# Expert lists of 32 tokens on four column strips in place of 64 tokens on two, in a fused float32 mixture-of-experts block

## The reference

```python
def hier_moe(x, w_group, b_group, w_expert, b_expert, w1, w3, w2):   # 256 tokens
    g_prob = softmax(x @ w_group + b_group)            # 4 groups, the best one is taken
    e_logits = (x @ w_expert + b_expert)               # 8 experts in that group, the best two are taken
    ...
    gates = sum(one_hot(expert_id, 32) * weight)       # two experts of 32 for each token
    def step(acc, ew):                                 # for each of the 32 experts
        h = silu(x @ w1e) * (x @ w3e)                  # 1024 -> 512
        return acc + ge[:, None] * (h @ w2e)           # 512 -> 1024
```

## Time and profile before

| | |
|---|---|
| median of 3 runs | 2823.86 us (2822.52 to 2825.3) |
| span of the profiled execution | 2819.0 us (no time of its own is given beside the span; the runs lie 3.5 to 6.3 us above it) |
| TensorE matmul busy | 2512.3 us, 89% |
| VectorE, ScalarE, GpSimd busy | 800.3, 628.9, 164.9 us |
| read from memory | 598.25 MB, of which expert weights 192 transfers of 2048 KB |
| experts, first layer | first up product at 248.05 us, last scatter ends at 795.21 us |
| experts, second layer | first up product at 1032.52 us, last scatter ends near 1531.9 us |

### The profile page before, as it was taken

One profiled execution on the slowest core, in us unless ns is written; L12 is line 12 of the kernel. 1 busy time (PEld: TensorE's weight loads), 2 busy tenths in 40 slices (PEclk: granted clock), 3 DMA queues, 4 the chain that ended last, 5 costly groups with the idle time before them and its releaser, 6 DMA issues.

```text
span 2819.0 us, 30761 instructions
## 1 busy us (share of the span) xinstructions
PE 2512.3 (89%) x12481; PEld 1598.0 (57%) x12482; DVE 800.3 (28%) x1338; ACT 628.9 (22%) x1012; POOL 164.9 (6%) x90
## 2 busy tenths in 40 slices
PE   7878999999979979999897897898999968878998
PEld 6544444444356644443333785556887847744996
DVE  1252011010020221011002546524232326354444
ACT  1121010101000610111102312423222224224334
POOL 0000000000000000000000325000000004240000
PEclk9988999999989989999999988899999988789999
DMA  8675976999966669999999001300323140130351
GB/s 326 260 276 187 393 286 231 393 393 394 396 250 243 233 242 385 394 393 393 395 396 359 1 1 60 123 1 22 113 90 120 45 163 1 60 117 7 135 199 71
DMA packets 241920, 602.27 MB, mean 214 GB/s; under 512 B 12679, under 2 KB 21751, under 8 KB 241824
## 3 DMA queue, kind: packets, MB, share of 16 engines
q1 hardware_dynamic: 241824, 600.91, 56.7%
HBM read 598.25 MB, written 2.64 MB: 213 GB/s over the span
## 4 chain that ended last, share of the span: by engine, by line
PE 70%; SPq 14%; DVE 6%; DMA 4%; ACT 2%; issue 2%; POOL 1%; DVEq 0%; ACTq 0%; POOLq 0%
PE ps L1756 13%; SPq L647 13%; PE ps L752 10%; PE ps L1565 8%; PE ps L1772 7%; PE ps L759 6%; PE ps L214 4%; PE ps L735 3%; PE ps L727 3%; PE ps L223 3%; PE ps L1738 3%; DMA ring<-in_moe_w_dram 1%; PE ps L1689 1%; PE ps L1709 1%; PE ps L313 1%
## 5 line engine op out<-in xcount | busy, mean ns | idle before, releaser
L752 PE MATMUL ps<-ring,arena 128*64 128x512 f32 x2176 | 477.2, 595 | 20.6 <-DMA ring<-in_moe_w_dram 18.7
L1756 PE MATMUL ps<-ring_r,ring_r 128*128 128x512 f32 (+1 forms) x2112 | 372.1, 339 | 12.5 <-DVE ring_r L2090 12.5
L1756 PEld LDWEIGHTS ps<-ring_r,ring_r 128*128 128x128 f32 x2112 | 329.0, 192 | 54.8 <-DVE ring_r L2090 13.1
L752 PEld LDWEIGHTS ps<-ring,arena 128*64 128x64 f32 x2176 | 155.9, 137 | 335.1 <-issue 305.8
L759 PE MATMUL ps<-ring,arena 128*64 128x512 f32 x1088 | 248.5, 598 | 26.8 <-ACT arena L817 13.8
L1565 PE MATMUL ps<-ring_r,ring_r 128*128 128x512 f32 (+2 forms) x1056 | 217.7, 367 | 8.9 <-DVE ring_r L1975 8.9
L1289 POOL TENSOR_TENSOR ring_r<-ring,ring_r 128x1024 fp32r<-128x1024 f32 (+2 forms) x28 | 85.9, 3088 | 2180.6 <-ACT ring_r L1284 2180.6
L1565 PEld LDWEIGHTS ps<-ring_r,ring_r 128*128 128x128 f32 x1056 | 189.1, 212 | 37.4 <-issue 9.3
L1772 PE MATMUL ps<-ring_r,ring_r 128*128 128x512 f32 x480 | 157.4, 401 | 12.3 <-DVE arena_r L1332 12.3
L759 PEld LDWEIGHTS ps<-ring,arena 128*64 128x64 f32 x1088 | 76.4, 137 | 151.2 <-issue 130.3
L907 DVE TENSOR_TENSOR arena<-ps,arena 128x512 f32<-128x512 f32 x34 | 23.6, 693 | 470.0 <-PE ps L752 470.0
(11 more groups left out here) (321 smaller groups left out, 2500.1 us busy)
## 6 DMA issues: line engine op xcount, KB each, us to landing
ring<-in_moe_w_dram SPq DMA_DIRECT2D x192, 2048.0 KB, 19.3
ring<-in_w_mod_dram SPq DMA_DIRECT2D x24, 2048.0 KB, 13.5
ring<-in_w_gate_dram SPq DMA_DIRECT2D x10, 2048.0 KB, 9.1
ring<-in_w_up_dram SPq DMA_DIRECT2D x10, 2048.0 KB, 14.2
ring<-in_w_in_dram SPq DMA_DIRECT2D x8, 2048.0 KB, 14.8
ring<-in_w_down_dram SPq DMA_DIRECT2D x8, 2048.0 KB, 11.4
ring<-in_w_out_dram SPq DMA_DIRECT2D x4, 2048.0 KB, 10.1
ring<-in_w_down_dram SPq DMA_DIRECT2D x4, 1536.0 KB, 8.1
```

The costliest lines, as they stand in the source:

```text
L752: ins = pe.matmul(PS[CAP * e:CAP * e + CAP, 2 + c, :], xeT[:, k, CAP * e:CAP * e + CAP], w[c][:, e, k, :], start=(k == 0), stop=(k == KT - 1))
L1756: ins = pe.matmul(PS[:, 2 * (i % GU_BANKS) + a, 0:ntok], w[:, k, a, :], as_r(x[:, k, 0:ntok]), start=(k == 0 and n == 0), stop=(k == KT - ...
```

## The change

A round takes 32 tokens of each expert (`CAP = 32`). The up product has 32 stationary columns for each expert, and its 512 output columns are split into two halves of 256, so that two experts x two halves lie on four column strips of 32. The down product splits its 1024 output columns likewise into two halves of 512 on four strips, so `down` is one stage and Y is 128 x 512. The scatter has one strip of 32 rows (an expert and a half) for each product: four products at a time go to four banks, then, behind a wait for a semaphore (`scattered`), four more with the two experts exchanged. `gather` moves 64 columns in place of 128, writes one bank, and stands ahead of the whole down product. ScalarE alone copies `xeT`, VectorE alone copies `Y`. `rounds` has four comparisons more (up to 8 rounds of 32 in place of 4 of 64).

```diff
-    CAP = 64
+    CAP = 32
+    HALF = HIDDEN // 2
...
-            def scatter(last=False):
-                for tt in range(NT):
-                    for h in range(2):
-                        ins = pe.matmul(PS[:, 4 + 2 * tt + h, :], sgT[:, tt * P:(tt + 1) * P], Y[:, h * 512:(h + 1) * 512],
+            def scatter(strips, last=False):
+                for tt, e in enumerate(strips):
+                    for o in range(2):
+                        at = 64 * e + 32 * o
+                        ins = pe.matmul(PS[:, 4 + 2 * tt + o, :], sgT[at:at + 32, tt * P:(tt + 1) * P], Y[at:at + 32, :],
...
-                        ins = pe.matmul(PS[:, 2 + k // 4, (k % 4) * P:(k % 4 + 1) * P], X[:, tt, k * P:(k + 1) * P],
-                                        view(sel[:, tt, 0, 0:1], [1, P]), start=(tt == 0), stop=(tt == NT - 1))
+                        ins = pe.matmul(PS[:, 2, 2 * CAP * k:2 * CAP * (k + 1)], X[:, tt, k * P:(k + 1) * P],
+                                        view(sel[:, tt, 0, 0:1], [1, 2 * CAP]), start=(tt == 0), stop=(tt == NT - 1))
...
                         for e in range(2):
-                            ins = pe.matmul(PS[CAP * e:CAP * e + CAP, 2 + c, :], xeT[:, k, CAP * e:CAP * e + CAP], w[c][:, e, k, :],
+                            for o in range(2):
+                                at = 64 * e + 32 * o
+                                ins = pe.matmul(PS[at:at + CAP, 2 + c, 0:HALF], xeT[:, k, CAP * e:CAP * e + CAP],
+                                                w[c][:, e, k, o * HALF:(o + 1) * HALF], start=(k == 0), stop=(k == KT - 1))
...
-                scatter()
+                scatter((0, 1)).then_inc(s("scattered"), 1)
                 for tt in range(NT):
-                    ins = pe.transpose(PS[:, 0, tt * P:(tt + 1) * P], selg[:, tt, :], ident)
+                    ins = pe.transpose(PS[:, 0, tt * P:(tt + 1) * P], view(selg[:, tt, 0, 0, 0:1], [1, P]), ident)
                 ins.then_inc(s("sgT_ps"), 1)
+                pe.wait_ge(s("scattered"), g * 2 + (2 * layer + 1))
+                scatter((1, 0)).then_inc(s("scattered"), 1)
                 pe.wait_ge(s("h"), g + 1)
-                for k in range(4):
+                for k in range(2):
                     ins = pe.transpose(PS[:, 1, k * P:(k + 1) * P], hh[:, k * P:(k + 1) * P], ident)
                 ins.then_inc(s("hT_ps"), 1)
+                pe.wait_ge(s("sel"), g + (2 + layer))
+                gather()
                 pe.wait_ge(s("sgT"), g + (2 + layer))
                 pe.wait_ge(s("hT"), g + 1)
                 arrived(2)
-                down(0)
-                pe.wait_ge(s("sel"), g + (2 + layer))
-                gather()
-                down(1).then_inc(s("y"), 1)
+                down().then_inc(s("y"), 1)
...
                 act.wait_ge(s("sgT_ps"), g + (2 + layer))
+                act.wait_ge(s("scattered"), g * 2 + (2 * layer + 2))
                 act.copy(sgT, PS[:, 0, 0:256]).then_inc(s("sgT"), 1)
...
-                dve.tensor_tensor(hh, PS[:, 3, :], hs, ALU.mult).then_inc(s("h"), 1)
+                dve.tensor_tensor(hh, PS[:, 3, 0:HALF], hs, ALU.mult).then_inc(s("h"), 1)
...
-                dve.tensor_copy(Y[:, 512:D], PS[:, 1, :]).then_inc(s("y_dve"), 1)
+                dve.tensor_copy(Y, PS[:, 0, :]).then_inc(s("y_sb"), 1)
```

More of the change, by code:

```diff
@@ L629, in moe @@
         pm, rounds, base = area(16), area(16), area(17)
-        sel = area(256).rearrange("p (t e c) -> p t e c", t=NT, e=2)
-        selg = area(256).rearrange("p (t s) -> p t s", t=NT)
+        sel = area(2 * 2 * CAP).rearrange("p (t e c) -> p t e c", t=NT, e=2)
+        selg = area(256).rearrange("p (t e o c) -> p t e o c", t=NT, e=2, o=2)
         sgT = area(256)
[L633 to L636, removed]
+        xeT = area(KT * 2 * CAP).rearrange("p (k s) -> p k s", k=KT)
+        hs, hh = area(HALF), area(HALF)
+        hT = area(HALF).rearrange("p (j s) -> p j s", j=2)
+        Y = area(512)
         st = small[:, 192:204]
@@ L754, in up, with down @@
                     ins.then_inc(s(("h1", "h3")[c]), 1)
-                def down(h):
+                def down():
                     for k in range(4):
                         for e in range(2):
-                            ins = pe.matmul(PS[CAP * e:CAP * e + CAP, h, :], hT[:, k, CAP * e:CAP * e + CAP],
-                                            w[2][:, e, k, h * 512:(h + 1) * 512], start=(k == 0), stop=(k == 3))
-                    return ins
-                pe.wait_ge(s("xe_act"), g + 1)
@@ L763, in body @@
-                pe.wait_ge(s("xe_dve"), g + 1)
+                            for o in range(2):
+                                at = 64 * e + 32 * o
+                                mid = 64 * e + 32 * (k // 2)
+                                ins = pe.matmul(PS[at:at + CAP, 0, :], hT[:, k % 2, mid:mid + CAP],
+                                                w[2][:, e, k, o * 512:(o + 1) * 512], start=(k == 0), stop=(k == 3))
+                    return ins
+                pe.wait_ge(s("xe_sb"), g + 1)
@@ L764, in body @@
                 up(0)
                 up(1)
-                pe.wait_ge(s("y_act"), g + (1 + layer))
-                pe.wait_ge(s("y_dve"), g + (1 + layer))
-                scatter()
+                pe.wait_ge(s("y_sb"), g + (1 + layer))
+                scatter((0, 1)).then_inc(s("scattered"), 1)
                 for tt in range(NT):
-                    ins = pe.transpose(PS[:, 0, tt * P:(tt + 1) * P], selg[:, tt, :], ident)
+                    ins = pe.transpose(PS[:, 0, tt * P:(tt + 1) * P], view(selg[:, tt, 0, 0, 0:1], [1, P]), ident)
@@ L778, in body @@
                 arrived(2)
-                down(0)
-                pe.wait_ge(s("sel"), g + (2 + layer))
-                gather()
-                down(1).then_inc(s("y"), 1)
+                down().then_inc(s("y"), 1)
             pe.wait_ge(s("ctrl"), layer + 1)
-            for b in range(2):
-                ins = pe.matmul(PS[:, b, :], zeros[:, 0:P], zeros, start=True, stop=True)
-            ins.then_inc(s("y"), 1)
+            pe.matmul(PS[:, 0, :], zeros[:, 0:P], zeros, start=True, stop=True).then_inc(s("y"), 1)
             if layer:
@@ L794, in pe_ @@
             total = pe.value_load(ctrl[0:1, cB + PAIRS:cB + PAIRS + 1], min_val=1, max_val=128)
-            pe.wait_ge(s("y_act"), total + (1 + layer))
-            pe.wait_ge(s("y_dve"), total + (1 + layer))
-            scatter(last=True).then_inc(s("done"), 1)
+            pe.wait_ge(s("y_sb"), total + (1 + layer))
+            scatter((0, 1), last=True).then_inc(s("scattered"), 1)
+            pe.wait_ge(s("scattered"), total * 2 + (2 * layer + 1))
+            scatter((1, 0), last=True).then_inc(s("scattered"), 1)
         def act_(act):
@@ L898, in body @@
                 for tt in range(NT):
-                    ins = dve.tensor_tensor(selg[:, tt, :].rearrange("p (e c) -> p e c", e=2), sel[:, tt],
-                                            view(gates[:, tt, bass.ds(pair, 2)], [1, 2], [0, CAP]), ALU.mult)
+                    ins = dve.tensor_tensor(selg[:, tt], view(sel[:, tt, 0, 0:1], [CAP, 2], [0, 2], [1, CAP]),
+                                            view(gates[:, tt, bass.ds(pair, 2)], [1, 2], [0, 2], [0, CAP]), ALU.mult)
                 ins.then_inc(s("sel"), 1)
-                dve.wait_ge(s("xe"), g * 2 + (2 * layer + 2))
-                dve.tensor_copy(view(xeT[:, 4, 0:1], [1, 512]), PS[:, 3, :]).then_inc(s("xe_dve"), 1)
                 y_copy(g)
@@ L906, in body @@
                 dve.wait_ge(s("h3"), g + 1)
-                dve.tensor_tensor(hh, PS[:, 3, :], hs, ALU.mult).then_inc(s("h"), 1)
+                dve.tensor_tensor(hh, PS[:, 3, 0:HALF], hs, ALU.mult).then_inc(s("h"), 1)
             def y_copy(g):
                 dve.wait_ge(s("y"), g + (1 + layer))
-                dve.tensor_copy(Y[:, 512:D], PS[:, 1, :]).then_inc(s("y_dve"), 1)
+                dve.tensor_copy(Y, PS[:, 0, :]).then_inc(s("y_sb"), 1)
             for_rounds(dve, body)
             dve.memset(tm, 0.0).then_inc(s("sel"), 1)
-            y_copy(dve.value_load(ctrl[0:1, cB + PAIRS:cB + PAIRS + 1], min_val=1, max_val=128))
+            total = dve.value_load(ctrl[0:1, cB + PAIRS:cB + PAIRS + 1], min_val=1, max_val=128)
+            y_copy(total)
             dve_layer_norm(dve, link, lambda tt, h: PS[:, 4 + 2 * tt + h, :],
-                           lambda e, tt, h: e.wait_ge(s("done"), layer + 1),
+                           lambda e, tt, h: e.wait_ge(s("scattered"), total * 2 + (2 * layer + 2)),
                            lnp[:, 0:D], lnp[:, D:2 * D], lambda e: e.wait_ge(S("ln_in1"), 32 * layer + 32), (xr, st), ln_tag)
```

19 lines of the change are left out of this document (6 added, 13 removed).

## The result

The kernel after takes 2832.84 us (median of 9 runs, 2827.2 to 2837.37) against 2823.16 us (9 runs). The ratio is 1.0034, with a 95% interval of [1.0024, 1.0043]: 9.7 us slower. A second series of 12 runs on another chip gives 1.0035 [1.0024, 1.0046]. The profiled span is 2828.7 us in place of 2819.0.

What follows compares the result with a forecast made beforehand. It took transfers (32 us) to bound pairs of one round, TensorE (59.5 us) pairs of two. Holes +10.8, starts -6.7, ends -19.6 and 5c of 6 gave -9.5: 2823.9 becomes 2814 us, range 2801 to 2846.

Steps and rivals of the forecast that it cites:

- the sum: Whole kernel: holes +10.8, layer starts -6.7, layer ends -19.6, plus 5c: -15.5 + 5c, or -9.5 us.
- rival 2: Each round 1 to 2 us longer, by late `sel` or slow instruction issue: 2830 to 2846 us, chance 0.19.
- One round: First `up` product to the next round's on TensorE: 17.6 us in place of 29.75.
- rival 1: Scatter row strips don't run together: round 22.4 us, +67 in all, about 2891 us, chance 0.09.
- Number of rounds: Lists over 32 tokens take more rounds: 43 in both layers in place of 34.
- Holes of the first layer: Transfer gaps behind pairs 4, 5 and 6: 57.2 + c us in place of 47.
- c: Delay when TensorE's clock has fallen while it waited for weights: taken as 1.2 us, bounds 0 and 3.
- Holes of the second layer: Transfer gaps at second pairs of two rounds (8 and 11), none at single ones: 2.6 + 2c us.
- The ends of the layers: Last w2 to last scatter's end: 7.4 + c us in place of 17.2, twice.
- The clock: TensorE's clock falls while idle; third rival, in each wait: c 2.5 to 3, total -3 to 0 us, chance 0.12.

Runs made afterwards that it cites:

- a_straight: The kernel after with TensorE's code written out for all 16 pairs in both layers, no jump back: 2815.77 us against 2823.88 before, ratio 0.9973.
- a_straight_again: The kernel after with TensorE's code written out for all 16 pairs, run again on another chip: 2818.77 us against 2822.74 before, ratio 0.9988.
- b_loop8: The kernel before with TensorE's loop over 8 pairs written out in place of 4, no other change: 2831.14 us, ratio 1.0036.

## Why the prediction was wrong

The forecast was 2814 us (-9.5), measured was +9.7. Two terms of the sum failed, both in the second layer: the jump of TensorE's loop, which it left out (point 3), and the holes behind pairs of two rounds, which it put at 5 us (point 5). By its terms the first layer should have changed by -0.6 us, and its stretch changed by -1.0; the second by -9.0, and it changed by +9.9. The time lies in the range of rival 2 (2830 to 2846), but not for its reason: no round got longer.

1. **One round: right, slightly too dear.** 17.04 us against 17.6. Row strips at 1.07 us (the lower bound 1.06; I took 1.2), one `up` pair 6.91, `gather` 3.68, `down` 3.57. By the page's factor of 3.07 (the Trainium skill, "TensorE: Matmul & The Clock Gate", Measured speedup vs the span model) a half would be 1.12 us; the row agrees within 0.05. Row strips do run together, so rival 1 did not occur, and the round is shorter than forecast, so neither did rival 2.
2. **Number of rounds: right**, 43.
3. **The sum left out the jump of TensorE's loop.** This is the first step that failed. I counted every product and weight load (424 for a round in place of 284) and asked only whether they could be issued fast enough, not what it costs to go back over them. Undone in both layers it gives 17 us in one series and 13 in another (1.0034 to 0.9973, 1.0035 to 0.9988), by the stretches some 11 of them in the second layer. With it gone the kernel is 3 to 8 us faster than before, on the side that was forecast.
4. **Holes of the first layer: right, with luck.** 57.7 us against 57.2 + c. With the measured round of 17.04 the same account gives 53.3 + c; the hole behind pair 4 is 18.7 us where it then has 15.2 + c, at least in part for the reason in point 5. The 47 us of the kernel before were also too few: its windows from 410 to 430 and 470 to 490 us show 369 and 361 GB/s, 3 us more. These errors work against each other.
5. **Holes of the second layer: too small, the second step that failed.** Forecast 2.6 + 2c, that is 5, measured 21.7, and without the long jumps 17.6 (2.5, 3.1, 6.5, 3.0 and 2.5 in `a_straight`) or 14.7 (`a_straight_again`). I had the channel full until the next slot lands, 10.7 us behind w2, and a restart before that as hidden. w2 of pair 7 lands at about 1258.8 (w3 at 1248.12 and 10.7). The next slot's last transfer lands in sixteen parts, marked in the trace from 1266.96 to 1269.45, and over that time the rate sinks. The last `h1` of pair 7 comes at 1267.28, 8.5 us behind w2. The sum had 7.0 there and no c, but the clock was at 0.51 when w3 came, and c was 1.5. With 1.9 us for the start of a transfer, new bytes can flow from about 1269.2. So the old slot fades out before the new one has begun, and a hole of 2 to 3 us stays at each pair of two rounds:

```profile
1263.80:1266.00 2.20, 2.20 (x48) 1.34 (x44) 0.69 (x1) 0.00 (x0) 0.00 (x0) 1.00 1.05 387
1266.00:1267.00 1.00, 1.00 (x24) 0.61 (x20) 0.00 (x0) 0.00 (x0) 0.00 (x0) 1.00 0.81 299
1267.00:1268.00 1.00, 1.00 (x25) 0.62 (x20) 0.00 (x0) 0.39 (x1) 0.00 (x0) 1.00 0.42 164
1268.00:1269.00 1.00, 1.00 (x28) 0.57 (x23) 0.00 (x0) 0.00 (x0) 0.00 (x0) 1.00 0.42 119
```

   The cheaper round and this term work against each other; together with the ends of the layers they leave the kernel without long jumps near -5.5 in place of -9.5. In the second layer's stretch nothing of the forecast gain is left then (498.7 to 503.4 against 499.4 before).
6. **The ends of the layers: right, by two errors that cancel.** w3 of the last pair lands at 776.27 in the first layer and the last scatter ends at 795.40, so 8.4 us behind w2 (10.7 behind w3), forecast 7.4 + c, that is 8.6, before 17.2. `down` ends at 792.21, 5.2 behind w2, so c was 1.7 there, not 1.2; what follows took 3.2 in place of 3.9.

```profile
756.70 19.57 DMA ring<-in_moe_w_dram
776.32 5.87 PE ps L757 x64
...
794.21 1.19 PE ps L731 x8
```

7. **The clock**: it falls in the waits and is at 0.5 when weights arrive (0.51 over 1248 to 1252), as forecast. c was 1.5 to 1.7 where it was read, in place of 1.2. It can also fall inside a pair, which cost 3.3 us in the profile of `a_straight`. What it costs in all was not isolated; keeping it up in the last pair moved nothing measurable.

Open stay: whether the first layer's jumps cost 3 us (traces) or 6 (runs); why the loop's place decides near the limit; and what part of `b_loop8`'s loss is the jump.

## What to carry to other kernels

Splitting work into smaller rounds for a tail of the data is worth the product of two numbers, the time of a round and how many the data asks for: here 29.75 us x 34 against 17.04 x 43, of which only what sticks out behind the transfers counts. Where a change multiplies instructions inside a hand-unrolled loop, count the instructions between two jumps back as well as their time, and look at the branch in the sequencer's rows. Write a loop out before judging such a change: with TensorE's code written out this one comes to 0.9973 and 0.9988 of the kernel before. A smaller loop, two pairs in place of four, is the obvious other cure; it was not run.

## What was not expected of the hardware

- A jump back over 1210 or 1466 instructions of TensorE took 0.22 us, over 1722 some 3.3 to 3.9 us, over 1766 and more 6.0 to 7.2 us; near the limit, shifting the same loop by 360 instructions made it short again in one of two layers. The page's line for instruction transfers grew with it (70 packets before, 129 after).
- Four row strips of 32 rows with 512 moving columns in float32 ran at 1.07 us for eight instructions, change of shape included, while the same eight at full height take 3.63 us.
- A transfer of 2 MB lands in sixteen parts, spread here over 2.5 us (1266.96 to 1269.45), and the rate sinks from 387 to 299, 164 and 119 GB/s meanwhile. The channel is not full until the landing.
- The granted clock fell to 0.71 and 0.67 in the middle of a pair's work in one profile of a kernel (`a_straight`) and not in the other of the same kernel.
